# Three orders of steps in place of one for the second pair of mixers, with exponentials behind their scores

## The reference

```python
u = rms_norm_2(h, norm_attn[i]) @ w_in[i]
o_a = nsa_attention(...)       # compressed, selected and window attention, 4 heads
o_b = diff_attention(...)      # softmax map 0 - lambda * softmax map 1
o_c = gla_mixer(...)           # gated linear attention, chunkwise
o_d = hgrn2_mixer(...)         # the same recurrence with other gates
h = h + concatenate([o_a, o_b, o_c, o_d]) @ w_out[i]
```

## Time and profile before

| | |
|---|---|
| Median of 3 runs | 2521.26 us (2514.09 to 2523.51) |
| The profiled execution | 2524.58 us |
| its span | 2522.8 us (1.8 us lie around it) |
| TensorE busy in it | 2479.1 us |
| mean granted clock | 0.988 of full speed |

### The profile page before, as it was taken

One profiled execution on the slowest core, in us unless ns is written; L12 is line 12 of the kernel. 1 busy time (PEld: TensorE's weight loads), 2 busy tenths in 40 slices (PEclk: granted clock), 3 DMA queues, 4 the chain that ended last, 5 costly groups with the idle time before them and its releaser, 6 DMA issues.

```text
span 2522.8 us, 47503 instructions
## 1 busy us (share of the span) xinstructions
PE 2479.1 (98%) x21555; PEld 1468.7 (58%) x21555; DVE 682.3 (27%) x1393; ACT 464.7 (18%) x789; POOL 136.1 (5%) x333
## 2 busy tenths in 40 slices
PE   9999999999999999999999999999999999999999
PEld 8766557866555776888445775344444534353444
DVE  3533633434543543111014433011010101011012
ACT  1522321432323533000014432000000000000001
POOL 5011000011000310000001200000000000000000
PEclk9999999999999999999999998999999999999999
DMA  7522343422235413444436213999999999999992
GB/s 244 151 85 68 101 133 134 146 94 68 94 108 146 157 35 105 137 163 150 154 127 164 100 62 136 389 403 389 387 394 377 377 388 389 409 371 394 394 381 96
DMA packets 194431, 542.32 MB, mean 215 GB/s; under 512 B 29200, under 2 KB 61360, under 8 KB 194224
## 3 DMA queue, kind: packets, MB, share of 16 engines
q1 hardware_dynamic: 180576, 536.82, 58.2%
q10 hardware_dynamic: 13344, 1.35, 0.4%
q0 software_dynamic: 304, 1.05, 0.1%
HBM read 538.12 MB, written 1.05 MB: 214 GB/s over the span
## 4 chain that ended last, share of the span: by engine, by line
PE 94%; DVE 3%; ACT 1%; issue 1%; DMA 0%; ACTq 0%; DVEq 0%
PE psum L2723 23%; PE psum L407 18%; PE psum L2736 12%; PE psum L2338 8%; PE psum L710 7%; PE psum L1488 5%; PE psum L2359 4%; PE psum L1670 3%; PE psum L472 1%; PE psum L2224 1%; PE psum L2781 1%; PE psum L2774 1%; PE psum L1026 1%; PE psum L1030 1%; PE psum L1957 1%
## 5 line engine op out<-in xcount | busy, mean ns | idle before, releaser
L407 PE MATMUL psum<-ring,hT 128*128 128x512 f32 (+3 forms) x1120 | 469.8, 571 | 4.4 <-ACT area L829 2.7
L2723 PE MATMUL psum<-ring,mix 128*32 128x448 f32 x4608 | 438.7, 539 | 0.2 <-DVE mix L2985 0.2
L407 PEld LDWEIGHTS psum<-ring,hT 128*128 128x128 f32 x1120 | 207.1, 190 | 214.2 <-issue 190.5
L2723 PEld LDWEIGHTS psum<-ring,mix 128*32 128x32 f32 x4608 | 148.9, 110 | 282.6 <-issue 280.8
L2338 PE MATMUL psum<-hT,ring 128*128 128x256 f32 x896 | 193.7, 379 | 0.0
L2338 PEld LDWEIGHTS psum<-hT,ring 128*128 128x128 f32 x896 | 170.1, 190 | 23.0
L710 PE MATMUL psum<-hT,ring 128*128 128x256 f32 x768 | 166.4, 379 | 0.0
L710 PEld LDWEIGHTS psum<-hT,ring 128*128 128x128 f32 x768 | 145.9, 190 | 20.7 <-issue 1.0
L2736 PE MATMUL psum<-area 128*32 128x256 f32 x2688 | 148.2, 379 | 0.9 <-DVE area L2976 0.9
L2974 DVE TENSOR_TENSOR area<-area,psum 128x1344 f32<-128x1344 f32 x16 | 24.6, 1535 | 457.6 <-PE psum L2723 457.6
L2723 PE MATMUL psum<-area,mix 128*32 128x448 f32 x1536 | 147.3, 539 | 0.0
(11 more groups left out here) (530 smaller groups left out, 2425.1 us busy)
## 6 DMA issues: line engine op xcount, KB each, us to landing
ring<-in_w_in_dram SPq DMA_DIRECT2D x88, 1024.0 KB, 5.1
ring<-in_moe_w_gate_dram SPq DMA_DIRECT2D x96, 896.0 KB, 6.9
ring<-in_moe_w_up_dram SPq DMA_DIRECT2D x96, 896.0 KB, 7.6
area<-in_moe_w_down_dram SPq DMA_DIRECT2D x112, 512.0 KB, 5.8
ring<-in_moe_w_down_dram SPq DMA_DIRECT2D x112, 512.0 KB, 6.2
area<-in_moe_w_gate_dram SPq DMA_DIRECT2D x32, 896.0 KB, 7.3
area<-in_moe_w_up_dram SPq DMA_DIRECT2D x32, 896.0 KB, 6.8
ring<-in_w_out_dram SPq DMA_DIRECT2D x16, 1024.0 KB, 5.1
```

What stands on the lines that cost most here:

```text
L407: last = nc.tensor.matmul(acc(g)[:, t, 0:d["n"]], lhs(kk, t), w[:, k, :], start=kk == 0, stop=kk == d["nk"] - 1)
L2723: last = nc.tensor.matmul(PS[32 * j:32 * j + 32, 3 * p + b, 0:PIECE].rearrange("p (m n) -> p m n", n=32), tokens(k, b), w[:, :, j, :], sta ...
```

## The change

`MIXER_PLAN` becomes three strings, one for each engine, with a common opening which is also the opening of the string before. `ATTN_ORDER` is changed: e3 stands right behind t2 (before: behind s4), e4 behind s4 alone, and e5 right behind s5 (before: behind s6). Every generator is advanced as often as before, so the instructions of each engine are the same ones in another order.

```diff
--- before.py
+++ after.py
@@ -1703,7 +1703,10 @@
             r = slice(f % P, f % P + 32)
             return TT[r, 5 + f // P, :], TT[r, 7 + f // P, :]
 
-        MIXER_PLAN = "cgfencfgcfngcfvgcfagfccgfacgfdafcaadfgdefaagafagfaagfaaafgaafgfafafagafaavgfffafapgpvgpp"
+        OPENING = "cgfencfgcfngcfvgcfagfccgfacgfdafca"
+        TENSOR_PLAN = OPENING + "adfgfdgaafagafaagafaafagafgfafafaafagagffafagfg"
+        SCALAR_PLAN = OPENING + "adfgdefaagafagfaagfaaafagaffagfafaafaagvffagfapgpfvgpp"
+        VECTOR_PLAN = OPENING + "adgdaagaagaagaaaagaagaaaagaagapgpgpp"
 
         def blended(plan, **parts):
 
@@ -1912,8 +1915,8 @@
                      (0, "diff", 1, 0), (1, "diff", 1, 1))
         OUTS_OF = ((0, 0), (1, 1), (2, 2), (3, 4), (5, 6))
         ATTN_ORDER = (("scores", 0), ("exp", 0), ("turn", 0), ("scores", 1), ("outs", 0), ("exp", 1), ("scores", 2),
-                      ("turn", 1), ("outs", 1), ("exp", 2), ("scores", 3), ("turn", 2), ("outs", 2), ("scores", 4),
-                      ("exp", 3), ("exp", 4), ("turn", 3), ("scores", 5), ("outs", 3), ("scores", 6), ("exp", 5),
+                      ("turn", 1), ("outs", 1), ("exp", 2), ("scores", 3), ("turn", 2), ("exp", 3), ("outs", 2),
+                      ("scores", 4), ("exp", 4), ("turn", 3), ("scores", 5), ("exp", 5), ("outs", 3), ("scores", 6),
                       ("exp", 6), ("turn", 4), ("outs", 4))
 
         def score_maps(i):
@@ -3297,7 +3300,7 @@
                     norm_act(s, n)
                 n += 1
                 u_act(s, L)
-                blended(MIXER_PLAN, g=gla_act(s, L), c=cmp_act(s, L), a=attention_act(s, L), n=heads_act(s, L),
+                blended(SCALAR_PLAN, g=gla_act(s, L), c=cmp_act(s, L), a=attention_act(s, L), n=heads_act(s, L),
                         d=diff_heads_act(s, L), f=fill_act(s, L), v=gates_act(s, L), e=gla_exps(s, L), p=post_act(s, L))
                 mix_act(s, DEPTH + L, 1)
                 norm_act(s, n)
@@ -3348,7 +3351,7 @@
                                 .then_inc(sem("x_updated"), 1), "x_updated")
                 n += 1
                 u_dve(s, L)
-                blended(MIXER_PLAN, g=gla_dve(s, L), c=cmp_dve(s, L), a=attention_dve(s, L), n=heads_dve(s, L),
+                blended(VECTOR_PLAN, g=gla_dve(s, L), c=cmp_dve(s, L), a=attention_dve(s, L), n=heads_dve(s, L),
                         d=diff_heads_dve(s, L), p=post_dve(s, L))
                 residual_dve(s, "out2", L, n, GAINC[:, 32 + 8 * L:40 + 8 * L])
                 norm_dve(s, n, GAINC[:, 32 + 8 * L:40 + 8 * L])
@@ -3397,7 +3400,7 @@
                 norm_rest_pe(pe, n)
                 u_pe(pe, L, fresh_from(n))
                 n += 1
-                blended(MIXER_PLAN, g=gla_pe(pe, L), c=cmp_pe(pe, L), a=attention_pe(pe, L), n=heads_pe(pe, L),
+                blended(TENSOR_PLAN, g=gla_pe(pe, L), c=cmp_pe(pe, L), a=attention_pe(pe, L), n=heads_pe(pe, L),
                         d=diff_heads_pe(pe, L), f=fill_pe(pe, L))
                 mix_pe(pe, "out2", L, DEPTH + L, n)
                 norm_rest_pe(pe, n)
```

## The result

| | before | changed |
|---|---|---|
| median of 6 runs | 2519.9 us | 2503.3 us |
| range | 2514.1 to 2524.3 us | 2497.6 to 2507.1 us |
| ratio of changed to before | | 0.9926 (0.991 to 0.9942) |
| ratio in a second comparison | | 0.9913 (0.9897 to 0.993) |
| profiled execution: its span | 2522.8 us | 2505.3 us |

The changed kernel is 16.6 us faster in the first comparison and 22.9 us in the second. I forecast 12.2 us. The median of the first comparison lies inside the stated range; that of the second, 2500.5 us, lies just under its lower end of 2501. The two profiled executions differ by 17.5 us of span.

The account below looks back on a forecast made before the run. TensorE, busy 98% of the span, was taken as the bound. Closing its holes was to give 10.2 us and the clock 2.0 us, so 2521.3 - 12.2 = 2509 us, range 2501 to 2519.

Parts of the forecast that it names:

- t1: Transposes on TensorE that wait for ScalarE's exponentials: a hole of 1.4 us stays, gain 0.
- g10 behind L2247: TensorE's unit g10 waits for a ScalarE copy queued behind an exponential: a new hole of 0.8 us.
- the first product: Product behind the transposes of the mixed outputs: ScalarE's copy comes late, hole 2.15 us in place of 1.22.
- d2: Transpose on TensorE waiting for VectorE's norm: a quarter put ahead covers the wait, gain 1.33 us.
- The end has a quarter among its thin steps: 1 us less in each (-2): Clock term at each layer's end: the low-clock stretch costs 1 us less per layer, -2 us together.
- the stretch at t1: Low-clock stretch following thin work and the hole at the transposes t1, 3.4 us in layer 0: forecast to remain.
- the thin run behind s6: s6, g13 and g14 without a quarter for 6.3 us: layer 0 gets a low-clock stretch as layer 1 has, +1.7 us.
- signs of being wrong that I had named: Wrong if t1's hole closed, t4 waits over 0.5 us, or low stretches total under 20 or over 45 us.
- The wait moves: Rival: TensorE's list takes the same 78 us because ScalarE ends last; 4 us won, 2517 us, chance 0.15.
- The clock follows the holes: Rival: with low-clock stretches gone or cut, the clock returns 8 us on top of 10.2; 2503 us, chance 0.12.
- stretch at 1493.9 us: Low-clock stretch in layer 1 after o3, g13 and s6, no hole ahead; the clock rival has it gone.
- Slower: Rival: new runs of thin steps keep the clock down; 16 us lost against 10.2 won, 2527 us, chance 0.05.

Follow-up runs that it names:

- vector_g9: The changed kernel with g9 ahead of o1 in VectorE's list; ratio 0.9916 to the kernel before, 2500.6 us.
- front_only: The kernel before with only the first group of TensorE's list reordered, from the first moved quarter to g9 ahead of o1; ratio 1.0001, 2519.3 us.
- old_tail: The changed kernel with the end of TensorE's and ScalarE's lists as before; 2512.3 us, ratio 0.9961 to the kernel before.
- all_four: The changed kernel with three edits closing its remaining holes, and f5.0 between g13 and g14 on TensorE; 2491.0 us, ratio 0.9881 to the kernel before.
- tail_only: The kernel before with only the new tail: f5.2 behind t4, f5.3 behind g15, ScalarE's copy of piece 5 later; ratio 1.0014, 2525.8 us.
- e1_early: The changed kernel with e1 ahead of g7 in ScalarE's list; 2503.3 us, ratio 0.9924 to the kernel before.
- copy_first: The changed kernel with ScalarE's last norm steps and the first product's copy ahead of piece 5's copy and v2; 2501.4 us, ratio 0.9928 to the kernel before.
- middle_only: The kernel before with two quarters moved on TensorE alone: f3.1 behind t2, f3.2 ahead of s4; 2511.6 us, ratio 0.9964.

## Why the prediction came out as it did

*The holes: right, step by step.* I forecast 10.2 us and the trace gives 10.1. The three that stay were named with their releasers: t1 (1.4 forecast, 1.19 measured), g10 behind L2247 (0.8 and 0.91) and the first product (2.15 and 2.28), 4.35 against 4.37 us. d2, o2, s4, f4.0, t3, t4, the unit's value product and the transposes wait no longer. vector_g9 showed that g10's hole is VectorE's order of g9 and o1, as the walk had it; front_only that the first group by itself gives nothing.

*The clock: the mechanism was right in part, the terms mis-sized.* I took -2.0 us. The profile gives -7.4 us, with 1.4 us lost by chance in the opening, so -8.8 us in the parts that I had forecast. Low stretches from s1 to the product's end, with half their length as an estimate of their cost:

| place | low us before (layers 0, 1) | low us changed | cost | forecast |
|---|---|---|---|---|
| t1 | 3.4, 3.4 | none | -3.4 | 0 |
| g10, t2 | none | 0, 3.4 | +1.7 | +1.7 |
| o2, s4 | 3.4, 3.4 | none | -3.4 | -3.4 |
| s6, g13, g14 | 0, 3.4 | 6.8, 6.8 | +5.1 | +1.7 |
| end and product | 6.8, 10.2 | none | -8.5 | -2.0 |
| sum | 34.1 | 17.1 | -8.5 | -2.0 |

The step that failed most is "The end has a quarter among its thin steps: 1 us less in each (-2)". It gave the end 2 us, where the stretch went whole. The changed kernel was run again to see whether that is chance: in none of its four profiled layers was there a low stretch at the end, and old_tail puts the tail at 9 us, all of it clock. Two smaller errors of 3.4 us cancelled each other: I kept the stretch at t1, which was gone in all four layers, and I gave the thin run behind s6 a stretch of 3.4 us, where it was 6.8 us long (two quarters, f5.0 and f5.1, took 5.44 us there) in three of the four layers and missing in the fourth. So one of the signs of being wrong that I had named did come: the low stretches add up to 17.1 us in the first profile and 13.7 us in the second, under 20. The median of the first comparison fell inside the range although the account of the clock did not hold.

*The price of low clock: the Trainium skill was nearer than my rows.* I had charged 14.9 us to the 34 us of low stretches, leaving out TensorE's idle time in them. all_four now shows the same work at full clock: 72.3 us from s1 to the product with 1.2 us idle, so 71.1 us of work, and 29.3 us of product. Layer 0 before took 86.2 - 9.5 - 71.1 = 5.6 us more and 1.4 us in the product, layer 1 88.3 - 9.3 - 71.1 = 7.9 and 2.2: 17.1 us in all. The rule quoted from the Trainium skill, "TensorE: Matmul & The Clock Gate", "Terms", gave an estimated 17. By that rule, the traces agree.

*The rivals.* "The wait moves" is refuted by three holes in place of nine. "The clock follows the holes" is half true. The median of the first comparison is its 2503 us, but not because holes closed: old_tail has closed them and kept the low time. Its stretch at 1493.9 us did not go either. "Slower" did not come: t1 with g9 had no low stretch in the four layers profiled, and the run of s6, g13 and g14 cost 6.8 us of low clock in three of them, which the end outweighed. The sum of the parts run alone (0.9964, 0.9985, 1.0001, 1.0014, together -0.36%) is half of the whole (-0.74%, -0.87%). The tail needs the early exponentials, and I did not see that before tail_only. Two parts were never run alone: t3 ahead of g12, and f4.3 and s6 ahead of g13.

*Open.* Why e1_early, vector_g9 and copy_first have up to 12 us more low time than the changed kernel, with nothing thin put together, was not settled. Each moves the later steps by 1 to 2 us against the low stretches, whose places also move between executions of one kernel. The profiled execution of e1_early has 13.7 us of low stretches from s1 to the product's end, no more than the changed kernel's 17.1 and 13.7. And whether the two short holes at the end or the thin steps between them bring the clock down was not parted.

## What to carry to other kernels

When the bound engine's list is reordered, walk it once against the other engines' lists: that walk gave each hole to 0.2 us. Then read the granted clock as a second account. In this kernel it fell behind runs of thin steps, with a hole beside them (o2 and s4) or without one (s6, g13, g14), and dense work put between g15 and g16 kept it up even where nobody needed the work. Test a part of a reordering inside the changed kernel too, not only alone: the tail was worth 9 us there and nothing alone.

## What the runs showed of the hardware that I had not expected

The opening of the mixers, the same instructions with the same waits ahead of it, took from 46.7 to 54.1 us, by the low stretches alone (3.4 to 13.7 us long, 3.4 to 20.5 us of them together). Take away TensorE's idle time (0.3 us or none) and half of the low time, and all 28 openings profiled come to 43.8 to 44.8 us. Among the 30 runs of the kernel before in one comparison, the mean granted clock ran from 0.984 to 0.990 and the time from 2528 to 2515 us. A low stretch ahead of a wait can hide the wait (middle_only at t1), so holes and low time should be counted together.
